# Two raw weight slots in place of three in a float32 transformer kernel on one core

## The chip, the cores and the metric

The kernel runs on one core of a Trainium2 chip. The metric is the device time of one execution in microseconds (us). Before the change the median of three runs is 2003.98 us.

## The reference

All data are float32, for 256 tokens of width 1024. A first block has two layers: a gated delta-rule layer (8 heads, chunks of 64 tokens) and an attention layer (8 heads, rotary positions), each followed by a layer norm and a SwiGLU feed-forward of width 2816. A second block takes its result and a context of 256 tokens. It computes modulation vectors from two condition vectors and a 1024 x 9216 matrix, runs a half feed-forward on latents and on context, then a token mixing (Fourier mixing and a two-directional mLSTM with 4 heads, joined by gates), and a last half feed-forward on the latents. Cut to its frame:

```python
x = first_block(x, ...)          # layer 0: gated_deltanet, layer 1: moba_attention
ml, mc = ada_params(c, w_ada, b_ada), ada_params(c_ctx, w_ada, b_ada)
h_lat = half_ffn(x,   ml[0], ml[1], ml[2], g[0], g[1], w13_a, w2_a)
h_ctx = half_ffn(ctx, mc[0], mc[1], mc[2], g[0], g[1], w13_a, w2_a)
h_lat = token_mixing(h_lat, h_ctx, ml[3:6], mc[3:6], ..., w_in, w_four, w_mproj, w_out)
return half_ffn(h_lat, ml[6], ml[7], ml[8], g[4], g[5], w13_b, w2_b)
# swiglu(u, w13, w2): a, b = split(u @ w13); (silu(a) * b) @ w2
```

## The kernel before

The activations stay in SBUF; the weights are streamed once each from HBM, in chunks of 128 x 2048 float32 (1 MB). There are 247 chunks that are multiplied in three products each: a float32 value is cut into a high part (a cast to a narrower float format) and a low part (the rest), for weights and activations, and PE sums high x high, high x low and low x high. Another 36 chunks, of the modulation matrix (`ada`), are multiplied raw by PE, 16 small matmuls each.

A chunk passes four stations. SP issues its load as two DMAs of 512 KB into a slot of `raw` (line 361, `load_stream`); ScalarE casts the high part into a slot of `whi` (line 368, `cut_hi`); VectorE subtracts and writes the low part into `wlo` (line 374, `cut_lo`), which is the last reader of the raw slot; PE multiplies (lines 397, 422, 439 by the kind of product). `raw`, `whi` and `wlo` each have `RING` = 3 slots. A load waits for the low cut (or, for `ada`, PE's use) of the load that had the slot before; a high cut waits for the landing and for PE's use of the cut three chunks earlier. Of a chunk `c`, the cut of `c + 3` (`cut_ahead`) stands in ScalarE's and VectorE's program at the place where they handle PE's result of `c`. Each engine goes through its program in order, so a cut that waits holds up what comes after it on its engine. SP does nothing but these loads, in the order of the list `LOADS`.

The order of the chunks is that of the `order` list: `g_qkv` (12), `g_z` (4), `g_out` (4), then `up0` (22) and `down0` (11), `m_qkv` (12), `m_out` (4), up and down 1, 2 and 3, `c_k`, `c_v`, `l_k`, `l_v`, `l_q` (4 each), `l_f` (2), `l_o` (4), `l_br` (8), `four` (4 of half size), `mproj` (4), `w_out` (4), `up4` and `down4`. The 36 `ada` loads go after the third chunk of `g_out`, so that loads 0 to 18 are cut chunks, 19 to 54 are `ada`, and 55 is the last chunk of `g_out`. Load 66 is chunk 10 of `up0`; loads 136, 138, 140 and 143 are chunk 9 of `down1` and chunks 0, 2 and 5 of `up2`; loads 241 to 245 are chunk 3 of `four` and chunks 0 to 3 of `mproj`.

At the start ScalarE and VectorE cut chunks 0 to 2 before anything else (`start_cuts`), then ScalarE casts the parameter columns (line 530) and the transposed input to `ah` (line 565), VectorE makes `al` (line 571) and cuts the small gate weights (lines 806 and 808), and PE begins with the gate products. In `down1` PE transposes the context tokens after the fourth chunk; POOL, ScalarE and VectorE turn them into the next `ah` and `al`. After `down1` VectorE does the layer norm's sums and rows (lines 604 to 647) before it goes on with `up2`. In `up2`, at chunk 5, ScalarE issues a bias row and the gate columns on its own DMA queue. In `four` VectorE scales each result (line 2222) and cuts; in `mproj` it multiplies (line 2230), adds (line 2232), ScalarE casts (line 2185) and cuts the chunk three ahead, then VectorE cuts and writes `al` (line 2235); `w_out` starts after the fourth such turn.

Of the kernel before, what the change touches and what calls it, by code (L numbers as in the profile page):

```python
# [17 lines left out]
F32 = mybir.dt.float32  # L18
# [5 lines left out]
P = 128  # L24
# [10 lines left out]
CC = 256  # L35
CHUNK = KD * CC
RING = 3

G_HEADS = 8
G_CHUNK = 64  # L40
# [102 lines left out]
def wait_from(eng, sem, value):  # L143

    if not isinstance(value, int) or value > 0:
        eng.wait_ge(sem, value)


def build(nc, A, out):
# [5 lines left out]
    def sb(name, shape, dt=F32):  # L155
        return ctx.enter_context(nc.sbuf_tensor(name, shape, dt))

    raw = sb("raw", [P, RING, CHUNK])
    whi = sb("whi", [P, RING, CHUNK], F32R)
    wlo = sb("wlo", [P, RING, CHUNK], F32R)  # L160
    ah = sb("ah", [P, KD, T], F32R)
# [45 lines left out]
    def S(name, value=None):  # L207

        old, ended = TAKES_OVER.get(name, (name, 0))
        if old not in sems:  # L210
            sems[old] = ctx.enter_context(nc.semaphore(old))
        return sems[old] if value is None else (sems[old], value + ended)
# [100 lines left out]
    for c, (q, j) in enumerate(CUTS):  # L313
# [5 lines left out]
        if q.evicted:  # L319
# [3 lines left out]
            else:  # L323
                ring = (ring + 1) % RING
                b = ring
            q.bank[j], q.last_in[j] = b, last_in.get(b)
            last_in[b] = (q, j)

    at_g_out = segs["g_out"].cut[0] + RING
    LOADS = CUTS[:at_g_out] + [(ada_w, j) for j in range(ada_w.n)] + CUTS[at_g_out:]  # L330
# [20 lines left out]

    def load_stream(sp):
        for r, (q, j) in enumerate(LOADS):
            if r >= RING:
                last, i = LOADS[r - RING]
                if last is ada_w:
                    sp.wait_ge(*S("ada_used", i + 1))
                else:
                    sp.wait_ge(*S("lo_ready", last.cut[i] + 1))
            for dst, src in q.src(j, r % RING):  # L360
                sp.dma_start(dst, src).then_inc(S(f"landed{r % RING}"), 16)

    def cut_hi(act, c):
        q, j = CUTS[c]
        r = place[q.name, j]
        act.wait_ge(*S(f"landed{r % RING}", 32 * (r // RING) + 32))
        wait_from(act, *S("used", c - RING + 1))
        act.copy(whi[:, c % RING, :], raw[:, r % RING, :]).then_inc(S("hi_ready"), 1)  # L368

    def cut_lo(dve, c):  # L370
        q, j = CUTS[c]
        r = place[q.name, j]
        dve.wait_ge(*S("hi_ready", c + 1))
        dve.tensor_tensor(wlo[:, c % RING, :], raw[:, r % RING, :], whi[:, c % RING, :].bitcast(F32),  # L374
                          ALU.subtract).then_inc(S("lo_ready"), 1)

    def cut_ahead(eng, c):

        if c + RING < len(CUTS):
            if eng is nc.scalar:  # L380
                cut_hi(eng, c + RING)
            else:
                cut_lo(eng, c + RING)

    def start_cuts(eng):
        for c in range(RING):
            if eng is nc.scalar:
                cut_hi(eng, c)
            else:
                cut_lo(eng, c)  # L390
# [99 lines left out]
    for g, members in enumerate(groups):  # L490
        r = 0
# [991 lines left out]
    def ada_chunk_pe(pe, j):  # L1483

        part, kk = j // 4, j % 4
        r = place["ada", j]
        pe.wait_ge(*S(f"landed{r % RING}", 32 * (r // RING) + 32))
        if j == 0:
            pe.wait_ge(*S("silu_c", 2))
        if kk == 0:  # L1490
            wait_from(pe, *S("ada", part - 1))
            if part == 1:
                pe.wait_ge(*S("cum", 1))
        w = raw[:, r % RING, :].rearrange("p (k n) -> p k n", k=2)
        for h in range(2):
            for i in range(4):
                last = pe.matmul(ada_bank(part)[32 * i:32 * i + 32, 0:256], silu_c[:, 2 * kk + h, :],
                                 w[:, h, 256 * i:256 * i + 256], start=(kk == 0 and h == 0),
                                 stop=(kk == 3 and h == 1))
        last.then_inc(S("ada_used"), 1)  # L1500

    def ada_bank(part):
        return ps[(3, 7)[part % 2]]
# [8 lines left out]
    def ada_pe(pe, j):  # L1512

        ada_chunk_pe(pe, j)
        if j % 4 == 1 and j > 4:
            ada_cols_pe(pe, (j - 5) // 4)
# [734 lines left out]
    @block.sync  # L2251
    def _(sp):
        load_stream(sp)
# [252 lines left out]
```

## Time and profile before

| | before |
|---|---|
| median of 3 runs | 2003.98 us (2003.22 to 2004.59) |
| profiled execution: its own time | 2002.6 us |
| profiled execution: span | 2000.8 us |
| mean granted TensorE clock | 0.932 |
| PE busy | 1799.9 us (90%) |
| VectorE busy | 1008.5 us (50%) |
| ScalarE busy | 747.9 us (37%) |
| DMA moved | 306.73 MB, mean 153 GB/s |

The span is from the first to the last instruction of the program. An engine's share of busy time says how much it works, not whether it is waited for. Matmuls are pipelined, so the durations of neighbours overlap, and the pace of a chunk is read from the starts. A timeline row has the start, the duration, the engine, the line, the operation, its output and inputs, their shape, the count, and in brackets the idle time of the engine before it and who ended that time. Neighbouring instructions of one kind are merged into one row. SPq is SP's queue; its row is an issue and not the transfer.

### The profile page before, as it was taken

To read this page: it belongs to the slowest core of one execution; us is meant where nothing else is said; L and a number is where in the kernel's file an instruction comes from. 1 tells how busy PE (TensorE), PEld (TensorE's weight loads), DVE (VectorE), ACT (ScalarE), POOL (GpSimd) and SP (SyncE) were. 2 spreads that over 40 slices of the span, in tenths; PEclk is the share of its full clock that TensorE was granted. 3 is DMA by queue.
4 is the path that set the end of the run, shared out by engine and by line. 5 is a ranking of instruction groups with operands and counts; after the bars stand their busy time and mean duration, and the time that the engine had idled before them with its cause. 6 is when DMAs were issued, how large, how long until landed. Compare 5 with 4: busy or idle time off the path is not lost. (4 is left out here: it accounts for less than half of the span.)

```text
span 2000.8 us, 28634 instructions
## 1 busy us (share of the span) xinstructions
PE 1799.9 (90%) x12218; PEld 1624.2 (81%) x12218; DVE 1008.5 (50%) x1200; ACT 747.9 (37%) x922; POOL 270.6 (14%) x225
## 2 busy tenths in 40 slices
PE   5996978989997857999999999999798899959998
PEld 5993847679986746998899899989587789949996
DVE  2743233355546435555665555555556454654553
ACT  2540211234432442443444444435344234434442
POOL 0106243130003003000210020002000110010000
PEclk8988988989998968999999999999799899979999
DMA  5554434656554503665676576554325024435652
GB/s 183 176 182 168 148 137 157 188 151 181 181 197 137 189 2 104 181 180 188 178 213 179 170 199 185 175 188 147 105 71 182 1 85 138 167 107 154 182 189 87
DMA packets 328835, 306.73 MB, mean 153 GB/s; under 512 B 12001, under 2 KB 286854, under 8 KB 328582
## 3 DMA queue, kind: packets, MB, share of 16 engines
q1 hardware_dynamic: 323168, 294.69, 48.2%
q10 hardware_dynamic: 5270, 9.18, 1.3%
q8 instruction: 97, 1.59, 0.3%
q0 software_dynamic: 272, 1.05, 0.1%
q14 instruction: 28, 0.23, 0.0%
HBM read 303.83 MB, written 1.05 MB: 152 GB/s over the span
## 5 line engine op out<-in xcount | busy, mean ns | idle before, releaser
L374 DVE TENSOR_TENSOR wlo<-raw,whi 128x2048 fp32r<-128x2048 f32 x247 | 578.6, 2344 | 453.7 <-ACT whi L368 453.6
L397 PE MATMUL ps<-ah,whi 128*128 128x256 f32 x2432 | 697.1, 287 | 23.5 <-DVE al L571 20.2
L397 PE MATMUL ps<-al,whi 128*128 128x256 f32 x2432 | 693.0, 285 | 0.0
L397 PE MATMUL ps<-ah,wlo 128*128 128x256 f32 x2432 | 692.8, 285 | 0.0
L368 ACT CAST whi<-raw 128x2048 fp32r<-128x2048 f32 x247 | 470.4, 1906 | 261.5 <-PE ps L422 156.8
L397 PEld LDWEIGHTS ps<-ah,whi 128*128 128x128 f32 x2432 | 472.4, 194 | 27.1 <-DVE al L571 21.4
L397 PEld LDWEIGHTS ps<-al,whi 128*128 128x128 f32 x2432 | 472.3, 194 | 1.6 <-issue 1.4
L397 PEld LDWEIGHTS ps<-ah,wlo 128*128 128x128 f32 x2432 | 471.9, 194 | 0.0
L708 ACT ACTIVATE f_sig<-ps 128x256 f32<-128x256 f32 x110 | 42.3, 384 | 367.5 <-PE ps L397 367.5
L422 PE MATMUL ps<-whi,fh 128*128 128x512 f32 x440 | 171.5, 390 | 0.0
L422 PE MATMUL ps<-wlo,fh 128*128 128x512 f32 x440 | 171.2, 389 | 0.0
L422 PE MATMUL ps<-whi,fl 128*128 128x512 f32 x440 | 171.2, 389 | 0.0
L737 DVE TENSOR_TENSOR f_act<-ps,f_sig 128x256 f32<-128x256 f32 x110 | 46.6, 424 | 152.5 <-ACT f_sig L708 152.5
L439 PE MATMUL ps<-whi,ah 128*128 128x512 f32 x256 | 103.0, 402 | 18.5 <-DVE al L2235 8.0
L439 PE MATMUL ps<-wlo,ah 128*128 128x512 f32 x256 | 101.9, 398 | 0.0
L439 PE MATMUL ps<-whi,al 128*128 128x512 f32 x256 | 101.8, 398 | 0.0
L422 PEld LDWEIGHTS ps<-whi,fl 128*128 128x128 f32 x440 | 82.6, 188 | 17.3
L422 PEld LDWEIGHTS ps<-wlo,fh 128*128 128x128 f32 x440 | 82.6, 188 | 17.0
L422 PEld LDWEIGHTS ps<-whi,fh 128*128 128x128 f32 x440 | 82.6, 188 | 16.8
L439 PEld LDWEIGHTS ps<-whi,ah 128*128 128x128 f32 x256 | 49.6, 194 | 31.3 <-DVE al L2235 8.8
L593 POOL TENSOR_TENSOR tadd<-tadd,adat 128x512 f32<-128x512 f32 x20 | 22.5, 1138 | 372.9 <-DVE tadd L581 372.9
L439 PEld LDWEIGHTS ps<-wlo,ah 128*128 128x128 f32 x256 | 49.7, 194 | 10.3
(338 smaller groups left out, 1955.4 us busy)
## 6 DMA issues: line engine op xcount, KB each, us to landing
raw<-in_f_w SPq DMA_DIRECT2D x132, 512.0 KB, 4.4
raw<-in_w_a SPq DMA_DIRECT2D x132, 512.0 KB, 4.6
raw<-in_w_ada SPq DMA_DIRECT2D x72, 512.0 KB, 4.5
raw<-in_w_in SPq DMA_DIRECT2D x68, 512.0 KB, 4.6
raw<-in_w_b SPq DMA_DIRECT2D x66, 512.0 KB, 4.5
raw<-in_a_w_in SPq DMA_DIRECT2D x32, 512.0 KB, 5.0
raw<-in_b_w_qkv SPq DMA_DIRECT2D x24, 512.0 KB, 4.4
raw<-in_a_w_out SPq DMA_DIRECT2D x8, 512.0 KB, 4.1
```

The source lines that it names most:

```text
L368: act.copy(whi[:, c % RING, :], raw[:, r % RING, :]).then_inc(S("hi_ready"), 1)
L374: dve.tensor_tensor(wlo[:, c % RING, :], raw[:, r % RING, :], whi[:, c % RING, :].bitcast(F32), ALU.subtract).then_inc(S("lo_ready"), 1)
L397: last = pe.matmul(out_ap, a, b, start=(i == 0), stop=(i == n - 1))
L422: last = pe.matmul(ps[4 + 2 * tt + h][:, :], x[:, k, cols_], y[:, kk, n], start=(k == 0 and i == 0), stop=(k == KF - 1 and i == 2))
L439: last = pe.matmul(ps[q.bank[first + tt]][:, :], x[:, 4 * half + kk, cols_], y[:, kk, :], start=(half == 0 and kk == 0 and i == 0), stop=( ...
L593: pool.tensor_tensor(v, v, shift(4 * (b % 2)).unsqueeze(2).to_broadcast([P, 4, P]), ALU.add).then_inc(S("shifted"), 1)
L708: act.activation(f_sig[:, j % RING, :], ps[b][:, 0:T], ACT.Silu).then_inc(S("silu"), 1)
L737: dve.tensor_tensor(f_act[:, j % RING, :], ps[b][:, T:2 * T], f_sig[:, j % RING, :], ALU.mult)\
```

## The change

`raw` gets a length of its own, `RAW` = 2 slots, and every index into it and every count of its landing semaphores goes by `RAW`. `whi` and `wlo` keep three slots. A load waits for the release of the load two places before it in `LOADS`, in place of three. `raw` shrinks by 8 KB in each partition, and nothing uses that room.

```diff
+RAW = 2
-    raw = sb("raw", [P, RING, CHUNK])
+    raw = sb("raw", [P, RAW, CHUNK])
...
     def load_stream(sp):
         for r, (q, j) in enumerate(LOADS):
-            if r >= RING:
-                last, i = LOADS[r - RING]
+            if r >= RAW:
+                last, i = LOADS[r - RAW]
                 if last is ada_w:
                     sp.wait_ge(*S("ada_used", i + 1))
                 else:
                     sp.wait_ge(*S("lo_ready", last.cut[i] + 1))
-            for dst, src in q.src(j, r % RING):
-                sp.dma_start(dst, src).then_inc(S(f"landed{r % RING}"), 16)
+            for dst, src in q.src(j, r % RAW):
+                sp.dma_start(dst, src).then_inc(S(f"landed{r % RAW}"), 16)
...
     def cut_hi(act, c):
-        act.wait_ge(*S(f"landed{r % RING}", 32 * (r // RING) + 32))
+        act.wait_ge(*S(f"landed{r % RAW}", 32 * (r // RAW) + 32))
         wait_from(act, *S("used", c - RING + 1))
-        act.copy(whi[:, c % RING, :], raw[:, r % RING, :]).then_inc(S("hi_ready"), 1)
+        act.copy(whi[:, c % RING, :], raw[:, r % RAW, :]).then_inc(S("hi_ready"), 1)
...
     def cut_lo(dve, c):
-        dve.tensor_tensor(wlo[:, c % RING, :], raw[:, r % RING, :], whi[:, c % RING, :].bitcast(F32),
+        dve.tensor_tensor(wlo[:, c % RING, :], raw[:, r % RAW, :], whi[:, c % RING, :].bitcast(F32),
                           ALU.subtract).then_inc(S("lo_ready"), 1)
...
     def ada_chunk_pe(pe, j):
-        pe.wait_ge(*S(f"landed{r % RING}", 32 * (r // RING) + 32))
+        pe.wait_ge(*S(f"landed{r % RAW}", 32 * (r // RAW) + 32))
...
-        w = raw[:, r % RING, :].rearrange("p (k n) -> p k n", k=2)
+        w = raw[:, r % RAW, :].rearrange("p (k n) -> p k n", k=2)
```

## Rows read from the trace of the kernel before

**Rows 1.** The page's shares of the span: busy us, share, instructions.
```profile
PE 1799.9 (90%) x12218; PEld 1624.2 (81%) x12218; DVE 1008.5 (50%) x1200; ACT 747.9 (37%) x922; POOL 270.6 (14%) x225
```

**Rows 2.** The waits of SP and PE: total us, times, longest.
```profile
SPq L361 <- DVE wlo L374: 1466.2, 244, 87.8
...
PE ps L397 <- DVE wlo L374: 2.5, 2, 1.5
```

**Rows 3.** Line 361 in three short windows: issues, then us to landing.
```profile
L361 SPq DMA_DIRECT2D raw<-in_a_w_in x2: 367/438/508, 18.4 to 18.8; - x2
...
DMA to landing us min/median/max: 4.0/4.5/5.0
...
L361 SPq DMA_DIRECT2D raw<-in_f_w x2: 368/476/583, 456.4 to 456.8; - x2
...
DMA to landing us min/median/max: 3.9/4.5/5.1
...
L361 SPq DMA_DIRECT2D raw<-in_f_w x2: 328/380/433, 954.5 to 954.9; - x2
...
DMA to landing us min/median/max: 3.5/4.0/4.5
```

**Rows 4.** Timeline of up0: VectorE, ScalarE and PE.
```profile
454.10 2.29 DVE L374 TENSOR_TENSOR wlo<-raw,whi 128x2048 fp32r<-128x2048 f32 x1 [1.34 <-ACT whi L368]
...
463.68 1.91 ACT L368 CAST whi<-raw 128x2048 fp32r<-128x2048 f32 x1
...
474.43 0.28 PE L397 MATMUL ps<-ah,whi 128*128 128x256 f32 x1
474.55 0.28 PE L397 MATMUL ps<-al,whi 128*128 128x256 f32 x1
```

**Rows 5.** Timeline of the start: VectorE, ScalarE and PE.
```profile
16.09 2.29 DVE L374 TENSOR_TENSOR wlo<-raw,whi 128x2048 fp32r<-128x2048 f32 x1 [16.09 <-ACT whi L368]
...
20.74 1.90 ACT L368 CAST whi<-raw 128x2048 fp32r<-128x2048 f32 x1 [1.27 <-DMA raw<-in_a_w_in]
...
27.97 0.35 PE L397 MATMUL ps<-swh,ah 128*128 128x16 f32 x1 [7.35 <-DVE swl L808]
```

**Rows 6.** Timeline of PE: modulation steps and the next work.
```profile
165.64 1.07 PE L1497 MATMUL ps<-raw,gb 128*32 128x256 f32 x16
...
171.47 1.07 PE L1497 MATMUL ps<-raw,gb 128*32 128x256 f32 x16
...
173.45 0.70 PE L1017 MATMUL ps<-diag,table 128*128 128x512 f32 x1 [0.53 <-POOL diag L1265]
```

**Rows 7.** Timeline from down1 to up2: ScalarE, VectorE and PE.
```profile
956.97 1.91 ACT L368 CAST whi<-raw 128x2048 fp32r<-128x2048 f32 x1 [3.00 <-PE ps L422]
...
978.73 1.91 ACT L368 CAST whi<-raw 128x2048 fp32r<-128x2048 f32 x1 [3.53 <-PE ps L422]
...
980.67 2.29 DVE L374 TENSOR_TENSOR wlo<-raw,whi 128x2048 fp32r<-128x2048 f32 x1 [3.15 <-ACT whi L368]
...
997.44 0.39 PE L397 MATMUL ps<-ah,whi 128*128 128x256 f32 x1 [1.54 <-DVE wlo L374]
```

**Rows 8.** Timeline of four, mproj and w_out's start.
```profile
1723.99 0.92 SPq L361 DMA_DIRECT2D raw<-in_w_mproj  x2
...
1724.48 2.53 DVE L374 TENSOR_TENSOR wlo<-raw,whi 128x2048 fp32r<-128x2048 f32 x1
...
1729.05 1.91 ACT L368 CAST whi<-raw 128x2048 fp32r<-128x2048 f32 x1 [2.87 <-DMA raw<-in_w_mproj]
...
1733.20 0.68 DVE L2230 TENSOR_TENSOR sig_b<-ps,sig_b 128x512 f32<-128x512 f32 x1
...
1760.18 0.79 PE L439 MATMUL ps<-whi,ah 128*128 128x512 f32 x1 [7.96 <-DVE al L2235]
```

**Rows 9.** Two windows where PE starts again: busy us of each engine, granted clock, DMA share, GB/s.
```profile
788.50:792.00 3.50, 3.50 (x16) 3.50 (x17) 3.50 (x1) 0.00 (x0) 3.50 (x2) 0.50 0.00 0
1760.20:1764.80 4.60, 4.60 (x11) 3.63 (x12) 0.00 (x0) 0.00 (x0) 0.00 (x0) 0.50 0.83 228
```

## The prediction, on record before the run

> **What bounds the kernel now.** I read the page's shares first, then the waits of SP and PE, then single loads by their issues and landings, then the places where PE stands still. TensorE is busy for 90% of the span [rows 1], so a change to the loads costs nothing until it makes PE wait, or makes ScalarE or VectorE late where PE waits for them. The SP queue stood for 1466.2 us in 244 waits on VectorE's low cuts (line 374), that is on a free raw slot; the queue is idle most of the time and loads run ahead. PE waited for a low cut twice in the whole run, 2.5 us in all [rows 2]. The landing of a raw chunk is therefore far from PE in nearly all 247 chunks, and the question is how far.
>
> **The steady pace.** In an up projection PE takes a chunk every 5.76 us (48 matmuls, 0.12 us from start to start [rows 4]). Take the chunk that PE starts at 474.43 [rows 4]. It is load 66. Its high cut starts on ScalarE at 463.68, as soon as PE has freed the cut slot; the low cut is done 4.23 us later, 6.5 us before PE wants it. The low cut of load 64 ends at 454.10 + 2.29 = 456.39, and SP issues at 456.4 [rows 3, 4]. Before, that release lets load 67 go; after the change the same release lets load 66 go. The second half is issued at 456.8 and lands 5.1 us later, so the megabyte is there at 461.9, 1.7 us (463.68 - 461.9) ahead of its high cut. Before, it went one pace of 5.76 us earlier. In the down projections the pace is 5.44 us (four high cuts from 956.97 to 978.73 [rows 7]) and the loads land sooner, 4.5 us after the second half's issue [rows 3]. So the removed slot costs 0 in the steady stretches. What hides it is PE's two chunks in the cut ring, and even a load late by 1 to 6 us would be taken up by the 6.5 us between low cut and PE. The loop of one slot, load 5.5 + high cut 1.9 + low cut 2.3 = 9.7 us, has to fit in two paces, 11.5 us. It does, so lateness melts by some 1.8 us in two chunks. Only if a load took over 7.3 us every time would the stream itself become the bound.
>
> **What the change adds, place by place.** No instruction is added or removed, all 566 issues stay; each load from the third on waits for the release of the load two before it in place of three. Behind a late load stand, on ScalarE, everything after its high cut, and on VectorE everything after its low cut. I went through the releases of all loads for those that land after their cut's present start. Most lie in front of slack. These do not:
>
> 1. The start. Load 2 now goes with the first issues; its high cut waits for the landing at 20.74, and the low cut, the casts to ah, VectorE's al and PE's gate products (27.97, after an idle time of 7.35 that VectorE ended) follow without a pause [rows 5]. After the change it waits for the low cut of load 0, done at 16.09 + 2.29 = 18.38. The load that is released there today is issued at 18.4 and 18.8 and lands 5.0 us later, at 23.8 [rows 3]. So the high cut starts at 23.8 in place of 20.74, and PE's first products are later by 3.1 us. Nothing covers this. I expect no gain from load 2 being out of the way, since it stands behind loads 0 and 1 in one queue; if loads 0 and 1 came 1 us sooner the cost would be 2.1, which is my lower end.
>
> 2. The modulation loads (36 chunks that PE reads raw, line 1497). PE leaves over 6 us between most of these steps, so a load issued two steps ahead is in time. From 165.64 on three steps come within 6 us. The load of the step at 171.47 is released by the step of 165.64, that is at 166.7; with 5.0 to 5.6 us to its landing it is there at 171.8 to 172.4, up to 0.9 late. 0.5 us of idle stand between it and the next work of the chain (173.45, [rows 6]). I take 0.4, bounds 0 and 0.9.
>
> 3. down1 into up2. Turning the tokens keeps ScalarE busy to 950, and the low cuts bunch up. The load of down1's chunk 9 goes at 954.5 as another does now, and lands at 954.9 + 4.5 = 959.4 [rows 3]; its high cut was at 956.97: 2.5 late. The lateness falls on every second chunk: up2 0 by 1.6, up2 2 by 0.5 to 0.8, at the high cut of 978.73 [rows 7]. Its low cut (980.67) is what VectorE does right before the layer norm's sums, and from there VectorE runs to the low cut for which PE waits at 997.44 (1.54 us of idle). So 0.5 us reach PE. Afterwards loads 143 to 149 land 3 to 5 us after their present cuts, since 143 is released only at 997.4. Followed chunk by chunk, the low cuts end 1.7 us or more before PE's need. I take 0.5 for this place; its upper end is 2.5, if landings slowed by the bias row and gate columns eat these 1.7 us. The same bunching in down2 and down3 ends in front of idle time or of 5 us of slack: 0.
>
> 4. four into mproj, the dearest with the start. four's chunks take PE only 3 us each, and three of mproj's loads decide. Today SP issues mproj 2 at 1723.99, released by the low cut of four 3, and it lands at 1729.05, where ScalarE waited for it; VectorE's low cut follows when the high cut of 1.91 us is done, and at 1733.20 its product of mproj 0, just when PE has finished that chunk [rows 8]. From here VectorE and ScalarE are a chain of four turns to PE's wait of 7.96 us at 1760.18. After the change the release at 1723.99 lets mproj 1 go: landed 1729.05, low cut 1730.99 to 1733.28, 0.35 us late for PE. mproj 2 goes at 1727.0 (the low cut of mproj 0, 1724.48 + 2.53) and lands 5.05 us later, at 1732.1. High cut to 1734.0, low cut to 1736.25. VectorE takes the product of mproj 0 then, and not at 1733.20: 3.05 late. mproj 3 goes at 1733.3, lands at 1738.35, 0.1 us after ScalarE could cut it. Sum 3.2 us, and all of it arrives at 1760.18. Lower end 2.6 (landings 0.5 sooner), upper end 3.8.
>
> 5. The last loads before the turn at 1415 arrive 1.4, then 0.2 us late: 0.2, bounds 0 and 0.5.
>
> Sum: 3.1 + 0.4 + 0.5 + 3.2 + 0.2 = 7.4 us; lower ends 4.7, upper ends (start 3.4) 11.1. The profiled execution took 2002.6 us by its own time, the median of the runs shown is 1.4 higher, so 2004.0 + 7.4 = 2011.4 us.
>
> The Trainium skill, DMA: Bandwidth & Descriptors, section "Anatomy of one DMA", fits a transfer as some 2.0 us fixed plus its bytes at 436 GB/s, measured on another issue path. For 1.05 MB that is an estimate of 4.4 us. The trace does not agree: 5.4 us from first issue to last landing at the start, 5.05 at mproj. By the page's figure the start would cost 2.1, mproj 2.4 and the whole some 5.
>
> **Rivals.** (a) Hidden anyway: the start's delay is taken up, because loads 0 and 1 land earlier without load 2 in flight, or the chunk chain of mproj has slack that I did not see. For it speaks PE's tiny wait for cuts [rows 2]; against it, the two places wait for the DMA or VectorE in the rows themselves. With either term gone the sum is 4.2 to 4.3, with more gone 1 to 3: 2005 to 2008.
>
> (b) The stream becomes the bound: load, high cut and low cut do not fit in two paces. Decides from a landing of 7.3 us in up, 6.7 in down. At 8 us the excess is 0.7 us in two chunks, some 90 us over the stream. The rows show 5.1 to 5.6 with one load in flight; after the change a slot's loads are no nearer to each other than that. A small form is likelier: stretches like up2 where several loads are late at once go over the margin of 1.7 to 6.5 us, another 5 to 15 us, 2017 to 2027.
>
> The Trainium skill, Perfetto Trace Analysis, "Optimization Strategy", has the same gap, repeated on the engine that should be full, as a sign of too few buffers. By that rule (b) would show as such gaps in the up projections; no row of before has them.
>
> (c) Faster: the clock. Each restart of PE after a pause is at half clock at first, for 3.5 us at 788.5 and 4.6 us at 1760.2 [rows 9]. If work shifts by 3 us against these changes, a restart can gain half of that difference, 0.55 us. The trace has 23 half-clock stretches; to outweigh 7.4 and win 4 more nearly all would have to gain. They will as often lose. 1996 to 2000, only if nearly all go one way and the two large terms are absent too.
>
> **Numbers.** Forecast 0.71 (2008.0 to 2015), (a) 0.14, (b) 0.12, (c) 0.03. 0.2%, or 4.0 us, is about what a measurement of this kernel can tell from no change. The forecast and (b) are slower by more, bar the lowest tail of the forecast. Slower 0.82, same 0.15, faster 0.03. The likeliest case's own range is 2008 to 2015; with (a)'s upper part and the beginning of (b), 2006.5 to 2017.
>
> **What would show it.** Right: the high cut of load 2 near 23.8, PE's gate products near 31.1; in up and down no wait of PE for a low cut beyond two or three at up2; loads landing 1 to 2 us ahead of their high cut there; PE's start of w_out 3.2 us later than the preceding shifts explain; SP's total wait for VectorE larger. Wrong: PE waits for line 374 repeated through the projections (b), or the start within 1 us of now (a).

## The result: 12 us slower, in a handful of places

The changed kernel takes 2016.32 us (median of 5 runs, 2012.91 to 2019.43) against 2004.00 us of the kernel before (2003.22 to 2004.59): the ratio is 1.0061, 95% interval 1.0048 to 1.0073. The forecast was 2011.4 us, slower by 7.4 us, with 2006.5 to 2017 as its whole range and 2008 to 2015 as that of its likeliest case. The profiled execution took 2014.51 us by its own time, 11.9 us more than that of before, and is the one read below. It stands in the lower half of the five runs.

The page's shares first, then the waits of SP, PE and ScalarE (total us, times, longest), which answer to [rows 1, 2]:

```profile
PE 1802.5 (90%) x12218; PEld 1626.2 (81%) x12218; DVE 1010.0 (50%) x1200; ACT 748.2 (37%) x922; POOL 269.9 (13%) x225
```

```profile
SPq L362 <- DVE wlo L375: 1484.9, 245, 87.4
...
PE ps L398 <- DVE wlo L375: 3.3, 2, 2.3
...
ACT whi L369 <- DMA raw<-in_w_a: 71.0, 24, 8.4
ACT whi L369 <- DMA raw<-in_w_in: 21.5, 5, 6.0
ACT whi L369 <- DMA raw<-in_a_w_in: 8.0, 3, 4.7
ACT whi L369 <- DMA raw<-in_f_w: 6.7, 2, 5.5
ACT whi L369 <- DMA raw<-in_w_mproj: 6.6, 2, 5.4
```

PE's work is the same and its waits for low cuts are still only two, 0.8 us longer. What is new stands one engine away: ScalarE now waits for landings, over 110 us in 36 waits, where before it did for 7.9 us in 4. Most of this costs nothing, as the prediction said: a high cut may be late as long as PE is still two chunks behind it. The steady pace shows it. The chunk that PE began at 474.43 before begins at 479.85 now, and every chunk of the stretch has the same 5.42 us. The load that the low cut ending at 456.1 lets go, its landing, and the high cuts of that time (answers to [rows 3, 4]):

```profile
L362 SPq DMA_DIRECT2D raw<-in_f_w x2: 368/706/1043, 456.1 to 456.5; - x2
...
DMA to landing us min/median/max: 3.8/4.7/5.7
```

```profile
463.34 1.90 ACT L369 CAST whi<-raw 128x2048 fp32r<-128x2048 f32 x1
...
469.10 1.91 ACT L369 CAST whi<-raw 128x2048 fp32r<-128x2048 f32 x1
```

This load is there at 462.2 and cut at 463.34, 1.1 us later, without a wait on the DMA; in up0 behind its first chunks the distance is 0.5 to 1.7 us, mostly about 1.5.

To see where the time came in, I took the first matmul of each chunk in both profiles. The table holds how much later than before PE comes to some of them, here and in the experiments below.

| PE's first matmul of | before, us | changed | w2_all | w2_but_start | w2_start_mproj | late_cut2 | w2_but_mlstm | w2_steady | late_cut3 | w2_but_ada_up2 | w2_mproj_only |
|---|---|---|---|---|---|---|---|---|---|---|---|
| g_qkv 0 | 38.20 | 3.05 | 3.31 | 0.10 | 3.19 | -3.39 | 3.19 | 0.00 | -3.10 | 2.97 | 0.08 |
| g_qkv 1 | 45.31 | 4.03 | 3.54 | 0.84 | 3.37 | -2.05 | 4.37 | 0.67 | -3.04 | 4.02 | 1.48 |
| g_out 3 | 396.16 | 5.51 | 3.84 | 1.96 | 3.27 | -0.64 | 5.62 | 1.15 | -2.88 | 4.99 | 0.09 |
| up2 0 | 978.47 | 5.38 | 3.92 | 1.88 | 3.57 | -0.35 | 5.87 | 1.44 | -2.90 | 5.30 | -0.04 |
| up2 3 | 997.44 | 6.19 | 4.71 | 2.86 | 3.56 | 0.41 | 6.39 | 1.43 | -2.91 | 5.29 | -0.04 |
| c_k 2 | 1381.56 | 7.70 | 6.23 | 4.41 | 3.55 | 0.45 | 6.41 | 1.41 | -2.94 | 5.25 | -0.04 |
| l_k 0 | 1467.58 | 8.93 | 9.84 | 7.75 | 3.53 | 2.48 | 8.40 | 1.41 | -2.97 | 8.25 | -0.05 |
| four 0 | 1715.30 | 8.37 | 10.45 | 8.41 | 3.59 | 2.94 | 9.10 | 1.51 | -2.94 | 8.68 | -0.50 |
| w_out 0 | 1760.18 | 11.31 | 13.53 | 11.74 | 6.76 | 6.04 | 12.13 | 1.46 | -3.00 | 11.81 | 2.66 |
| down4 10 | 1985.91 | 11.91 | 13.95 | 11.98 | 6.98 | 6.42 | 12.58 | 1.54 | -2.91 | 12.12 | 3.13 |

The changed kernel's column moves in steps: 3.05 at the start, 1.0 in PE's first chunk, 1.5 in the delta rule, 0.8 in up2, 1.5 in c_k, 1.2 before l_k, 3.0 at mproj and w_out, 0.6 behind them. Two steps go the other way: 0.1 before up2 and 0.6 between l_k and four, of which the cause is not known. From g_out to up2, through two whole feed-forwards and the attention, it stays within 0.15 us.

**The start.** The timeline of ScalarE and PE (answers to [rows 5]):

```profile
23.80 1.90 ACT L369 CAST whi<-raw 128x2048 fp32r<-128x2048 f32 x1 [4.66 <-DMA raw<-in_a_w_in]
...
31.02 0.35 PE L398 MATMUL ps<-swh,ah 128*128 128x16 f32 x1 [11.14 <-DVE swl L809]
```

The high cut is where it was forecast (23.8), and PE's gate products begin 3.05 us later. Then comes a term that the forecast did not have. Windows of PE's first real chunk, first the changed kernel and then the kernel before (busy us of each engine, granted clock, DMA share, GB/s):

```profile
41.10:46.40 5.30, 5.30 (x26) 5.30 (x26) 0.00 (x0) 0.00 (x0) 0.00 (x0) 0.50 0.01 3
```

```profile
38.20:41.10 2.90, 2.90 (x14) 2.90 (x15) 0.00 (x0) 0.00 (x0) 0.00 (x0) 0.50 0.03 6
41.10:46.40 5.30, 5.30 (x47) 5.30 (x46) 0.01 (x1) 0.88 (x3) 0.00 (x0) 1.00 0.00 0
```

Before, PE worked at the lower level (1.2 GHz, a granted clock of 0.50) for 2.9 us of the chunk, now for 5.2 (41.25 to 46.4). The difference of 2.3 us at half pace is some 1.1 us, of which 1.0 is seen.

**Modulation steps, up2, the turn before l_k.** PE's and ScalarE's rows at the places of [rows 6, 7] and before l_k:

```profile
140.13 1.93 PE L1498 MATMUL ps<-raw,gb 128*32 128x256 f32 x16 [4.23 <-DMA raw<-in_w_ada]
...
178.48 0.42 PE L1498 MATMUL ps<-raw,gb 128*32 128x256 f32 x4 [1.62 <-DMA raw<-in_w_ada]
...
984.95 1.90 ACT L369 CAST whi<-raw 128x2048 fp32r<-128x2048 f32 x1 [4.38 <-DMA raw<-in_w_a]
...
1003.63 0.38 PE L398 MATMUL ps<-ah,whi 128*128 128x256 f32 x1 [2.35 <-DVE wlo L375]
...
1424.12 1.90 ACT L369 CAST whi<-raw 128x2048 fp32r<-128x2048 f32 x1 [4.84 <-DMA raw<-in_w_in]
```

Each of them is a wait for a landing, or for the low cut behind one. The high cut of 984.95 is the chunk whose cut began at 978.73 before; less the 5.38 us that the kernel is late here, it is 0.84 us late, and so is PE at 1003.63, whose wait grows from 1.54 to 2.35 us.

**c_k.** Here no wait stands behind the 1.5 us. From the end of down3 to PE's second c_k chunk, PE does the gate products (16 columns each) and the first chunk without any idle time in all eleven profiles of the table. The windows of this work in the kernel before, in the changed kernel and in late_cut2, which has two slots as well:

```profile
1361.58:1375.80 14.22, 14.22 (x98) 14.22 (x96) 5.73 (x10) 7.22 (x13) 6.17 (x8) 0.76 0.46 149
```

```profile
1367.74:1383.50 15.76, 15.76 (x98) 15.76 (x96) 5.73 (x10) 7.22 (x13) 6.94 (x8) 0.68 0.45 149
```

```profile
1361.98:1376.25 14.27, 14.27 (x98) 14.27 (x96) 5.73 (x10) 7.22 (x13) 5.59 (x8) 0.76 0.49 158
```

The length times the granted clock is nearly the same, 10.7 to 10.9 us, so the whole step of 1.5 us is the clock's.

**mproj.** ScalarE, VectorE and PE (answers to [rows 8]; the kernel is 8.36 us late when it comes here):

```profile
1737.23 1.91 ACT L369 CAST whi<-raw 128x2048 fp32r<-128x2048 f32 x1 [5.42 <-DMA raw<-in_w_mproj]
1740.36 1.91 ACT L369 CAST whi<-raw 128x2048 fp32r<-128x2048 f32 x1 [1.22 <-DMA raw<-in_w_mproj]
...
1742.30 2.29 DVE L375 TENSOR_TENSOR wlo<-raw,whi 128x2048 fp32r<-128x2048 f32 x1 [0.24 <-ACT whi L369]
1744.51 0.69 DVE L2231 TENSOR_TENSOR sig_b<-ps,sig_b 128x512 f32<-128x512 f32 x1
...
1771.49 0.79 PE L440 MATMUL ps<-whi,ah 128*128 128x512 f32 x1 [7.88 <-DVE al L2236]
```

Two landings in a row hold ScalarE up. VectorE's product of mproj 0 comes at 1744.51; 1733.20 and 8.36 would be 1741.56, so it is 2.95 us late, and PE's w_out as well (11.31 against 8.36).

### The profile page after: what moved, and what is told of

Same layout as the page of the kernel before. It is cut to its first block and busy times, and to the rows that moved or that the text cites. A ratio compares the mean times of both kernels' runs of the same rounds, so it can differ in the third digit from the quotient of the medians.

```text
span 2012.7 us, 28634 instructions
## 1 busy us (share of the span) xinstructions
PE 1802.5 (90%) x12218; PEld 1626.2 (81%) x12218; DVE 1010.0 (50%) x1200; ACT 748.2 (37%) x922; POOL 269.9 (13%) x225
```

## The experiments

Rows of the table below with the same median of before were taken beside the same runs; the others are best compared by what they are over before. The kernels called w2_ have three raw slots in memory, and only the load that is waited for changes. Their edit is one line, with a different value for `back`:

```diff
     def load_stream(sp):
         for r, (q, j) in enumerate(LOADS):
-            if r >= RING:
-                last, i = LOADS[r - RING]
+            back = 2
+            if r >= back:
+                last, i = LOADS[r - back]
```

| kernel | `back`, or the edit | median us (lowest to highest, runs) | before beside it | ratio, 95% interval |
|---|---|---|---|---|
| w2_all | 2 | 2015.19 (2013.78 to 2016.53, 5) | 2003.13 | 1.0056, 1.0042 to 1.0069 |
| w2_but_start | 3 for load 2, else 2 | 2013.59 (2012.81 to 2014.59, 5) | 2003.13 | 1.0049, 1.0035 to 1.0062 |
| w2_start_mproj | 2 for loads 2 and 243 to 245, else 3 | 2009.40 (2007.48 to 2011.5, 6) | 2003.13 | 1.0029, 1.0017 to 1.0042 |
| late_cut2 | two slots, start reordered | 2010.72 (2008.32 to 2012.56, 6) | 2003.13 | 1.0037, 1.0025 to 1.0049 |
| w2_steady | 2 for 205 loads of the stream | 2004.30 (2002.53 to 2005.53, 11) | 2003.82 | 1.0001, 0.9992 to 1.0010 |
| w2_but_mlstm | 3 for loads 202 to 216, else 2 | 2013.49 (2013.07 to 2015.2, 5) | 2003.82 | 1.0046, 1.0032 to 1.0060 |
| raw1 | one slot | 3022.01 (3014.0 to 3030.03, 2) | 2003.82 | 1.5077, 1.5038 to 1.5116 |
| late_cut3 | three slots, start reordered | 2001.68 (1999.66 to 2002.38, 11) | 2003.82 | 0.9986, 0.9977 to 0.9995 |
| w2_but_ada_up2 | 3 for 19 to 57 and 136 to 150, else 2 | 2013.72 (2012.87 to 2014.73, 4) | 2003.40 | 1.0048, 1.0032 to 1.0063 |
| w2_mproj_only | 2 for loads 243 to 245, else 3 | 2007.04 (2005.49 to 2008.58, 11) | 2003.40 | 1.0016, 1.0007 to 1.0025 |

### w2_all: only the wait

The edit is the diff above.

> Three raw slots stay in memory, but every load waits for the release of the load two places before it. Theory A (the later release alone costs the time): the same as the changed kernel, 1.006 of before, about 2016 us, with PE's first chunk near 41.3 and w_out's start near 1771. Theory B (the place of the buffers in SBUF, or the reuse of one slot, has a part in it): clearly under 2016 us, at the limit that of before, 2004 us.

12.1 us over before, as the changed kernel's 12.3. The buffers lie where they lay before, so the place in SBUF and the reuse of a slot have no part that shows. The later release costs the time. The profile has its steps at the same places, but not all of the same size: from c_k 2 to l_k 0 it adds 3.6 us in place of 1.2, with a granted clock of 0.77 in place of 0.81 between c_v 3 and l_k 2.

### w2_but_start: the start's wait undone

```diff
+            back = 3 if r == 2 else 2
```

> As w2_all, but load 2 waits for nothing, as before. Theory A: only the start comes back, PE's first chunk at 38.2 in place of 41.25 and no longer half clock in the second chunk: 4 us less than w2_all, about 2012 us. Theory B (the delays overlap, and what is won at the start is lost again at the modulation loads): within 1 us of w2_all.

The start comes back: PE's gate products begin at 28.07 and its first chunk is 0.10 us from that of before, 3.2 us sooner than in w2_all. But the median is only 1.6 us under that of w2_all, and not 4. In the profiles 0.5 of the 3.2 us are gone by the second chunk, since PE's first chunk runs longer at half clock, and 0.8 more by g_out. Theory A is right on the place and was too sure of the sum; what is won at the start is partly given back by the clock.

### w2_start_mproj: the two dear places alone

```diff
+            back = 2 if r == 2 or 243 <= r <= 245 else 3
```

> Three raw slots and waits as before, except that load 2 waits for load 0 and loads 243 to 245 (mproj 1 to 3) for the load two places before. Theory A (a few places, of which these two are the dearest): 3.05 + 1.0 at the start and 3.0 at mproj, 7 us over before, about 2011 us; the projections run as before. Theory B (the loss is spread over the stream): 1 to 2 us over before.

6.3 us over before by the medians, 7.0 in the profile, for four loads of 283 that go later. In the profile the start gives 3.4 and mproj 3.2, and from g_out to four PE's lateness stays between 3.27 and 3.6 us over 1300 us. Theory A holds, theory B does not.

### late_cut2: the third cut moved behind the input's turn

```diff
-        start_cuts(act)
+        start_cuts(act, 0, 2)
         params_act(act)
         turn_act(act, 0)
+        start_cuts(act, 2, 3)
...
-        start_cuts(dve)
+        start_cuts(dve, 0, 2)
         turn_dve(dve, 0)
+        small_weight_cut(dve, 0)
+        start_cuts(dve, 2, 3)
         gdn_in_dve(dve)
```

with `small_weight_cut` taken out of `gdn_in_dve` and `start_cuts(eng, a, b)` over the chunks `a` to `b - 1`.

> The changed kernel with two raw slots, but the third of the first cuts stands behind the turn of the input and the cut of the gate weights on ScalarE and VectorE. Theory A (the start costs because the cut of chunk 2 stands ahead of the input's casts and waits for its load): PE's gate products start at about 25 us, and not at 31, and the whole is 5 to 7 us less than the changed kernel, 2009 to 2011 us. Theory B (the start is bound by the landing of the input, the parameters or the gate weights): PE's gate products stay at 28 us or later, 3 us less at most.

PE's gate products start at 24.58, so the input and the weights were there, and only the cut of chunk 2 had stood in front of them. The first chunk comes 6.4 us sooner than in the changed kernel, 6.1 by the second chunk. The median is 5.6 us under its 2016.32; each held against its own runs of before, it is 4.7 us (12.3 over, and 7.6 over), a little under the 5 that were expected. Theory A.

### w2_steady: 205 loads of the stream alone

```diff
+            back = 3 if r == 2 or 19 <= r <= 57 or 136 <= r <= 150 or 202 <= r <= 216 or 243 <= r <= 248 else 2
```

> Three raw slots; 205 of the 281 loads that wait (all but load 2, the modulation loads and those next to them 19 to 57, 136 to 150 around down1 and up2, 202 to 216 around c_k and c_v, 243 to 248 at mproj) wait for the load two places before. Theory A (the steady stream hides the lost slot): within 1 us of before, no wait of PE for a low cut beyond those of before. Theory B (the loss is spread over the stream): 3 us or more over before.

0.5 us over before, ratio 1.0001 with 1.0010 as the upper end: no difference, or at most 2 us. The waits of PE and ScalarE:

```profile
PE ps L398 <- DVE wlo L375: 2.5, 2, 1.5
```

```profile
ACT whi L369 <- DMA raw<-in_w_a: 30.6, 13, 8.2
```

PE's row is that of before to the digit, though ScalarE waits for 13 landings of one weight alone. No wait shows that the lost slot is paid for in the steady stream. The single profile is 1.5 us behind that of before all the same, and 1.4 of this is there by up2 (0.67 in PE's first chunk, where the changed loads have no part). The 21 runs of before differ among themselves by 3.3 us.

### w2_but_mlstm: the loads before l_k

```diff
+            back = 3 if 202 <= r <= 216 else 2
```

> As w2_all (every load waits for the load two before), but loads 202 to 216, the last of down3 to l_v, wait as in the kernel before. Theory A (the late high cuts of 206, 212 and 214 hold up what ScalarE does after them): PE's start of l_k (load 212) has no added lateness against its start of c_k's predecessors, 3 to 4 us less than w2_all. Theory B (it is the clock after the pause, which moves by itself): the same as w2_all within 1 us.

1.7 us under w2_all, 2.4 when each is held against its own runs of before: between the two theories, and the trace says why. The wait before the turned tokens is that of before (7.7 us; w2_all has 9.4 and the changed kernel 9.0), in the row of PE's waits:

```profile
PE ps L1908 <- DVE tadd L582: 7.7, 1, 7.7
```

So the landings do cost 1.3 to 1.7 us here. Yet from c_k 2 to l_k 0 PE falls back by 2.0 us (6.41 to 8.40). Two windows of the same work, PE's small products after the turn, here and in w2_start_mproj (granted clock in the column before the DMA share):

```profile
1436.80:1439.70 2.90, 2.90 (x15) 1.75 (x14) 0.68 (x1) 0.73 (x1) 0.00 (x0) 0.51 0.00 0
```

```profile
1434.00:1437.00 3.00, 2.05 (x19) 1.40 (x17) 1.49 (x4) 0.67 (x1) 0.00 (x0) 1.00 0.00 0
```

One has the lower clock and the other the full one. Both theories have a part. At c_k nothing is added (6.39 to 6.41), but this speaks for neither theory: w2_but_ada_up2 and late_cut2 add nothing there either, with the later loads.

### raw1: one slot, to see the loop as the bound

```diff
-RAW = 2
+RAW = 1
```

> One raw slot: a load waits for the release of the load just before it. By the loop of load 5.1 to 5.6, high cut 1.9, low cut 2.3 and 0.1 to 0.3 for hand-over a chunk takes 9.5 to 10 us against 5.4 to 5.8 now, so PE stands still in every chunk: some 3.9 to 4.3 us for each of 247, less what the cut ring takes up behind attention, the delta rule and the mLSTM, 900 to 1060 us more, 2900 to 3060 us. If the loop were not the limit of the slots, the time would stay under 2500 us.

3022 us, in the range. ScalarE in an up projection:

```profile
707.14 1.91 ACT L369 CAST whi<-raw 128x2048 fp32r<-128x2048 f32 x1 [7.54 <-DMA raw<-in_f_w]
...
716.98 1.90 ACT L369 CAST whi<-raw 128x2048 fp32r<-128x2048 f32 x1 [7.36 <-DMA raw<-in_f_w]
...
727.06 1.91 ACT L369 CAST whi<-raw 128x2048 fp32r<-128x2048 f32 x1 [7.61 <-DMA raw<-in_f_w]
```

In these rows a turn takes 9.84 and 10.08 us: the load from issue to last landing 5.7 (701.4 to 707.1), the high cut 1.9, the low cut 2.3. Two slots share such a loop between two chunks, 4.9 to 5.0 us each, under PE's 5.44 and 5.76; one slot doesn't. Here ScalarE waits for the landing in 235 of 247 chunks, and the wait reaches PE:

```profile
PE ps L398 <- DVE wlo L375: 336.3, 121, 7.3
```

That agrees with the rule on consistent bubbles of the Trainium skill, Perfetto Trace Analysis, "Optimization Strategy", which the prediction weighed for two slots; there the trace shows no such row. The expectation put the whole loss down to PE standing still. With the down projections and the other products PE waits 501.8 us for low cuts, in 186 waits, which is half of the 1018 us. The mean granted clock is 0.826 here and 0.932 before, so part of the rest is PE working slowly in the time that the loop leaves it.

### late_cut3: the reordered start on the kernel before

The same edit as late_cut2, on the kernel with three slots.

> The kernel before, with three raw slots, and the third of the first cuts behind the turn of the input and the cut of the gate weights. The two-slot form of this order began PE's chunks 3.4 us sooner than before; the same start here, and nothing else changed: 1.5 to 3.5 us less than before, about 2001 us. A rival: the clock gives it back, within 1 us of before.

PE's gate products start at 24.87, 3.10 us sooner, and 2.9 of this last to the end of the profile. By the medians it is 2.1 us, within the 1.5 to 3.5 expected, ratio 0.9986, interval 0.9977 to 0.9995: it beats both kernels, by less than the 0.2% that a single comparison can tell, but with 11 runs beside 21 the interval excludes 1.

### w2_but_ada_up2: the modulation loads and up2

```diff
+            back = 3 if 19 <= r <= 57 or 136 <= r <= 150 else 2
```

> As w2_all (every load waits for the load two before), but loads 19 to 57 (the modulation loads) and 136 to 150 (down1 into up2) wait as in the kernel before. Theory A: between g_z's last chunk and g_out, and at up2's chunk 3, nothing is added to PE's lateness (the changed kernel added 1.5 and 0.8 us there): 1.5 to 2.5 us less than w2_all, 2012.7 to 2013.7 us. Theory B (in these places the clock adds by itself what the loads do not): PE's lateness grows at g_out by 1 us or more all the same.

1.5 us under w2_all, 1.7 when each is held against its own runs of before. At up2 3 nothing is added (5.30 to 5.29; PE's wait is 1.52 us again), so the 0.8 us are the landings' doing. At the first modulation steps nothing is added either. But by g_out PE is 1.0 us later all the same, so the changed kernel's 1.5 us in the delta rule are no clean measure of the loads. Theory A holds for up2, theory B for the delta rule.

### w2_mproj_only: mproj alone

```diff
+            back = 2 if 243 <= r <= 245 else 3
```

> Waits as in the kernel before, but loads 243 to 245 (mproj 1 to 3) wait for the load two places before. Theory A (the landing of mproj 2 comes 3 us later and starts VectorE's chain of four turns that much later): PE's start of w_out 3.1 to 3.2 us later against the chunks before it, the whole 3 to 3.4 us over before, about 2007 us. Theory B (the two-slot waits at mproj cost only because the kernel comes there late): under 1 us.

3.6 us over before by the medians. ScalarE and PE at the place:

```profile
1728.41 1.91 ACT L369 CAST whi<-raw 128x2048 fp32r<-128x2048 f32 x1 [5.46 <-DMA raw<-in_w_mproj]
1731.52 1.91 ACT L369 CAST whi<-raw 128x2048 fp32r<-128x2048 f32 x1 [1.21 <-DMA raw<-in_w_mproj]
```

```profile
1762.84 0.80 PE L440 MATMUL ps<-whi,ah 128*128 128x512 f32 x1 [7.67 <-DVE al L2236]
```

The kernel comes to `four` 0.50 us sooner than before and leaves at w_out 2.66 later: 3.16 us, as the sum for mproj had it. Theory A.

## Why the prediction was right, and what it missed

The direction, the two large terms and the signs hold: the high cut of load 2 at 23.80, PE's gate products at 31.02, two waits of PE for low cuts, w_out 3 us late. The size holds only with luck. 2016.32 us lies outside the likeliest case's 2008 to 2015 and inside the whole range by 0.7 us, in the part that was added for the beginning of rival (b), and that rival's mechanism did not occur.

**The steady stream costs 0.** Right to within 0.1%, shown by w2_steady (1.0001, at most 1.0010) and by PE's unchanged rows. The loop that hides it is the one reckoned: 9.7 us by the prediction, 9.8 to 10.1 in raw1.

**Rival (a), hidden anyway.** It does not hold. In the profiles mproj costs its full 3.16 us when it is alone, the start its 3.2 in w2_start_mproj, and the start undone begins PE's work as early as before. By the medians undoing the start gave only 1.6 us, since the clock took part of it back.

**The start, 3.1.** Measured 3.05 to PE's first chunk, 2.97 to 3.31 in four other profiles that have this wait. Load 2 out of the way did not bring loads 0 and 1 sooner by more than 0.2 to 0.3 us (the low cut of load 0 starts at 15.90, 16.09 before). Load 2 landed 5.55 us after its first issue (18.22). The Trainium skill's fit (DMA: Bandwidth & Descriptors, "Anatomy of one DMA") gives an estimate of 4.4 us for these bytes, on another issue path; the trace does not agree, and the sum by it would have been farther off.

**The clock at the start.** Missed: another 1.0 us, in PE's first chunk. I had half-clock restarts only as a rival that could make the kernel faster.

**Modulation steps, 0.4.** The step named, at 171.47, did wait, for 1.62 us, and behind it PE was 1.2 us later than ahead of it; in w2_all it waited for 0.83 us and lost 0.4. The prediction overlooked the first step: its load, issued when chunk 17's low cut was done, left PE idle for 4.23 us in place of 2.78, the granted clock was 0.50 in place of 1.00, and the step took 1.93 us in place of 1.07. By the next step 1.1 us of this were left. With the clock in between, no net size can be given for the loads alone.

**up2, 0.5.** 0.84 us of lateness at the high cut and 0.8 at PE. Right in place and mechanism, 0.3 short; its upper end of 2.5 was not touched, since none of the loads from 143 on for which ScalarE waited made PE wait. The same bunching in up3 cost nothing, as forecast.

**The turn before l_k, 0.2.** Too small. The last of these loads (214) was issued at 1417.64 and landed 6.46 us later (6.46 to 6.54 in the five profiles where these loads wait for the load two before), against 5.52 us before and 5.60 in w2_but_mlstm. The high cut waited 4.84 us for it and began 1.3 us late in place of the 0.2 forecast, and PE's wait grew by 1.3 us, by 1.7 in w2_all. What makes this landing longer is not shown; the load before it had landed at 1416.29, and the load behind it was issued at 1421.64.

**c_k, no term.** The 1.5 us are the clock's, by the windows above. Three profiles with the later loads have them (the changed kernel, w2_all, w2_but_start), two with the same loads do not (late_cut2, w2_but_ada_up2). Whether a profile has them is not decided by the loads at this place.

**mproj, 3.2.** 3.0 in the changed kernel, 3.16 alone. Right.

**The sum.** 7.4 against 11.9 in the profile and 12.3 by the medians. Its large terms hold (3.1 and 3.2 for 3.05 and 3.0). The step that was too small is the last one, "Sum: 3.1 + 0.4 + 0.5 + 3.2 + 0.2": it had no term for the clock, and 0.2 stood where 1.3 was measured. In the profile about 3.1 us are the clock's: 1.0 at the start, 1.5 at c_k, 0.6 at w_out and up4. The delta rule, with the modulation steps, gave 1.5 for 0.4, in which loads and clock were not separated; up2 gave 0.8 for 0.5.

**Rival (c), the clock, with the other sign.** It did not make the kernel faster. But it is the part that no count of waits gives. The prediction tied it to restarts after a pause; at c_k it came with PE working without a pause. And single terms can't be had from medians to less than about 1 us.

## What to carry to other kernels

A buffer that is taken away is paid for where the stream starts or restarts and where an engine works on the critical path right behind a cut, not in the steady stretch; so look at the loads there, one by one, and let the loop of load and uses against the pace of the consumer answer for the rest. An operation that waits for a load should not stand ahead of work whose data is already there: moving the third cut behind the input's turn made the start immune to the lost slot and gained 2 us on the old kernel. When a change moves the moments at which PE restarts, allow for the clock on top of the sum; here it was about 3 us in the profile of the changed kernel.

## What the runs showed of the hardware that was not expected

The granted clock adds discrete amounts to the same work. From down3's last chunk to c_k 2 eight profiles took 25.4 to 25.5 us and three took 27.0, with no wait of PE in any. The clock fell to half there while PE did its 16-column gate products (at 1365.45 in the kernel before), and PE had not paused ahead of it. After the turn before l_k, PE's small products ran at 0.51 in one profile and at 1.00 in another, with the same waits ahead of them, and 2.0 us came in from there to l_k. The first big chunk had 5.2 us of half clock in one kernel and 2.9 in another. w2_mproj_only, whose start is that of before, came 1.48 us late to its second chunk, and was back at 0.09 by g_out. The runs of the changed kernel spread over 6.5 us (2012.91 to 2019.43) where the five of before had 1.4 us; but over 21 runs before had 3.3 us too (2002.14 to 2005.48), so how much of the wider spread is the landings' and how much the clock's stays open.
